# A decoder step on one core: two projections of the first group moved into the step-size chain, history rows written at once, first group written out on TensorE

## The chip, the cores and the metric

The kernel runs on one core of one Trainium2 chip. The metric is the device time of one launch in microseconds (us), the median of several runs; lower is better. Five engines work side by side, each on its own instruction stream and in its own order: TensorE (PE in the profile: matrix products; PEld is its weight load), VectorE (DVE), ScalarE (ACT), GpSimd (POOL) and SyncE (SP, which issues most DMA transfers). They meet at semaphores: an instruction can raise one when it ends, and an engine can wait until one has reached a number.

## The reference, cut to what matters

One layer of a hybrid decoder is computed in float32 for 256 prompt rows and 32 sample rows (8 sequences of 4), together 288 tokens, width 1024. The part that the change touches is the beginning:

```python
h = rmsnorm(x, lw['g_mix'])
proj = h @ lw['w_in']                       # 1024 -> 10272 columns
xbc, dt_raw = proj[..., o3:o4], proj[..., o4:o5]
xbc_c, ssd_buf = causal_dwconv(xbc, ssd_buf0, lw['ssd_conv_w'], lw['ssd_conv_b'])   # 4 taps, history of 3 rows
xbc_c = jax.nn.silu(xbc_c)
dt = jax.nn.softplus(dt_raw + lw['ssd_dt_bias'])
A = -jnp.exp(lw['ssd_A_log'])
a = dt * A;  cum = jnp.cumsum(a, axis=...)   # per chunk, 32 heads
decay_to_end = jnp.exp(cum[:, :, -1:] - cum)
```

An SSD recurrence, an RG-LRU recurrence and gates follow, then the branch and output products, a mixture of 16 experts, and the per-layer embedding gate. All of that is the same before and after.

## The kernel before, in words

The kernel has a prologue, a mixer of eight groups (G = 8), the branch products, the experts and an end. A group needs ten projections of 128 columns each (numbered 0 to 9; 10 and 11 are projections 0 and 1 of the next group). To get float32 accuracy from the faster matrix format, each 128-column weight block is split: ScalarE writes the high part, `whi` (helper `large`, L722), VectorE subtracts it to get the low part, `wlo` (helper `small`, L1007), and TensorE adds three products for each of eight row blocks (helper `proj`, 24 matmuls, L1464 to L1466). There are two `whi`, two `wlo` and two PSUM banks, so a projection waits for its own `wlo` and for the evacuation of the projection two places before it. ScalarE's helper `evac` waits for projection i, splits the weights of projection i+2 (`large`), and copies projection i into a padded buffer `pads[i]` (L752, L753), to which GpSimd adds the three history rows of the samples (L642). VectorE's `conv` then makes four passes over the padded buffer (L1072, L1074 twice, L1077), and ScalarE applies silu.

Every engine's order is fixed in the code. In the prologue, after the normalised input has been transposed and split, a chain makes the step sizes `dt` and what follows from them. It goes to and fro: VectorE adds the bias (L1014) and takes an absolute value (step "ax", L1016); ScalarE an Exp (step "z", L729); VectorE adds 1 (step "u", L1018); ScalarE an Ln (step "ln", L731, with a table load ahead of it); VectorE a correction with a reciprocal, up to `aT` (L1020 to L1028); TensorE transposes it (L1475, L1477); VectorE copies it out, step "atok" (L1030 to L1033); TensorE makes the running sums (L1482); VectorE copies them, `cumT`, and forms `dteT` (L1036 to L1041); ScalarE an Exp (step "dte", L733, again with a table load); TensorE transposes all into token order (L1489, L1490, step "tm"); VectorE copies that into `TM` (L1050, L1051, step "tm" of its own).

TensorE does projections 0 and 1 ahead of that chain and projections 2 to 9 behind it, in the loop over the groups. VectorE does `small` 0 and 1 ahead of the chain, and behind it small 2, conv 0, small 3, conv 1, small 4, conv 2 and so on. GpSimd waits for the end of the chain ("tm"), writes the five sets of history rows, and then computes `Dg`, a product of 64 x 1152 elements (L645), before it copies rows for the state output. ScalarE's and VectorE's programs have group 0 and group 7 written out and a loop over groups 1 to 6; TensorE's has a loop over groups 0 to 6 and group 7 written out.

Of the kernel before, what the change touches and what calls it, by code (L numbers as in the profile page):

```python
# [23 lines left out]
ACT = mybir.ActivationFunctionType  # L24
# [12 lines left out]
G = 8  # L37
# [118 lines left out]
def build(nc, a):  # L156
    with ExitStack() as ctx:
# [38 lines left out]
        u = sb("u", [P, T])  # L196
# [100 lines left out]
        sp = [arena[:, 4608 + 296 * i:4904 + 296 * i] for i in range(5)]  # L297
        aT = arena[0:H, 6249:6537]
        dteT = arena[0:H, 6537:6825]
# [55 lines left out]
        pe_pro = Steps(sem("pe_pro"), [f"x{k}" for k in range(KC)] + ["par", "hist", "rms", "dt", "atok", "cum", "tm"])  # L355
        act_pro = Steps(sem("act_pro"), [f"sq{k}" for k in range(KC)] + ["rs", "A"] + [f"hh{k}" for k in range(KC)] + ["z", "ln", "dte"])
# [272 lines left out]
        def _(pool):  # L629
# [3 lines left out]
            pool.wait_ge(dve_pro.sem, dve_pro.at("tm"))  # L633
            pool.wait_ge(pe_pro.sem, pe_pro.at("tm"))
            with pool.Fori(0, G) as g:
# [7 lines left out]

                pool.wait_ge(CU_ready.sem, CU_ready.at(g, -3))
# [51 lines left out]
        def _(act):  # L696
# [31 lines left out]
            act.wait_ge(dve_pro.sem, dve_pro.at("ax"))  # L728
            ch.step(act_f(sp[2], sp[1], ACT.Exp, scale=-1.0), act_pro, "z")  # L729
            act.wait_ge(dve_pro.sem, dve_pro.at("u"))  # L730
            ch.step(act_f(sp[4], sp[3], ACT.Ln), act_pro, "ln")  # L731
            act.wait_ge(dve_pro.sem, dve_pro.at("dteT"))
            ch.step(act_f(dteT, dteT, ACT.Exp), act_pro, "dte")  # L733

            act.sem_inc(silu_done.sem, 4)
            act.sem_inc(T_free.sem, 1)
            act.sem_inc(CB_free.sem, 1)

# [6 lines left out]
            def evac(g, i):  # L745

                act.wait_ge(projected.sem, projected.at(g, i + 1))
                large(g, i + 2)
                n = i % 10
                act.wait_ge(conv_done.sem, conv_done.at(g, i + 1 - 5 if i < 10 else n + 1))  # L750
                act.wait_ge(stashed.sem, stashed.at(g, i + 1 - 5 if i < 10 else n + 1))
                ch(act_f(pads[n][:, 3:SMP], bP[n % 2][:, 0:NP], ACT.Copy))  # L752
                ch.tell(act_f(new_tokens(pads[n], 3), samples(bP[n % 2][:, NP:T]), ACT.Copy), proj_free, i + 1)  # L753
# [4 lines left out]
            def group(g, first, last):  # L758
# [27 lines left out]
                evac(g, 2)  # L786
# [56 lines left out]

            evac(0, 0)
            evac(0, 1)
            ch.enter(0, 11)
# [124 lines left out]
        def _(dve):  # L971
# [31 lines left out]
            def small(g, b):  # L1003

                s = b % 10 % 5
                dve.wait_ge(w_large.sem, w_large.at(g, b + 1))
                v.tensor_tensor(wlo[b % 2][:], wflat(s), whi[b % 2][:].bitcast(F32), ALU.subtract).then_inc(w_small.sem, 1)  # L1007

            small(0, 0)
            small(0, 1)  # L1010

# [6 lines left out]
            ch.step(v.tensor_scalar(sp[3], sp[2], 1.0, None, ALU.add), dve_pro, "u")  # L1018
            dve.wait_ge(act_pro.sem, act_pro.at("ln"))
# [8 lines left out]
            ch.step(v.tensor_scalar(aT, sp[0][0:H, 0:T], Acol, -1.0, ALU.mult, ALU.mult), dve_pro, "aT")  # L1028
            dve.wait_ge(pe_pro.sem, pe_pro.at("atok"))
# [22 lines left out]
            dve.sem_inc(conv_done.sem, 5)  # L1052
# [33 lines left out]
            small(0, 2)  # L1086
            conv(0, 0, C_SW, 32, C_SB, 0)
            small(0, 3)
# [330 lines left out]
        def _(pe):  # L1419
# [52 lines left out]
            proj(0, 1)  # L1472
            pe.wait_ge(dve_pro.sem, dve_pro.at("aT"))
# [9 lines left out]
            ins.then_inc(pe_pro.sem, 1)  # L1483
            pe.wait_ge(act_pro.sem, act_pro.at("dte"))
# [11 lines left out]
            def group(g, last):  # L1496
# [53 lines left out]
                for i in range(2, 6):  # L1550
                    proj(g, i)
# [62 lines left out]
            with pe.Fori(0, G - 1) as g:  # L1614
                group(g, False)
            group(G - 1, True)
# [246 lines left out]
```

## Time and profile before

| What | Value |
|---|---|
| median of 3 runs | 1013.66 us (1012.64 to 1015.18) |
| the profiled execution: its own time, and its span in the trace | 1013.02 us, 1011.2 us |
| TensorE busy | 899.4 us (89%) |
| VectorE busy | 594.5 us (59%) |
| ScalarE busy | 411.9 us (41%) |
| GpSimd busy | 169.8 us (17%) |
| mean granted clock of TensorE | 0.937 of full speed |
| DMA | 188.54 MB, mean 186 GB/s |

Times in the trace run from the span's start; the 1.8 us between the span and the execution's own time lie outside the traced instructions. "Busy" is an average over stages with different limits, so what a change in one place is worth must be read from that place. The granted clock of TensorE has two levels here, 1.00 (2.4 GHz) and 0.50 (1.2 GHz). The end of a matmul is modelled, and successive matmuls overlap: their starts are the safer numbers.

### The profile page before, as it was taken

The numbers are of one execution on the slowest core, as the hardware profiler recorded it, in microseconds if no ns is written. First come the engines' busy times: TensorE is split into PE (matmuls) and PEld (weight loads), VectorE is DVE, ScalarE is ACT, GpSimd is POOL, SyncE is SP. The second block draws the span as 40 slices with busy tenths as digits, with TensorE's granted clock in tenths as the row PEclk, the third lists the DMA queues.
The fourth block names the chain that finished last, engine by engine and source line by source line (L and its number), as shares of the span: only waits on it lengthen the run. The fifth ranks groups of instructions, "written<-read, shape, count | busy, mean of one in ns | idle before, by whom it ended". The sixth has DMA issues, their size and how long they took to land.

```text
span 1011.2 us, 16515 instructions
## 1 busy us (share of the span) xinstructions
PE 899.4 (89%) x5345; PEld 680.0 (67%) x5345; DVE 594.5 (59%) x1092; ACT 411.9 (41%) x704; POOL 169.8 (17%) x214
## 2 busy tenths in 40 slices
PE   6588997988889897898959999998999999999986
PEld 3488887878788786887839997773444444444464
DVE  2786778788776877878776542345243252333534
ACT  2457564636647464575755331242111111111232
POOL 0045142342513324152310000020000000000000
PEclk9889998989979899997968999998999999999998
DMA  7154552727246172642718522954999999999201
GB/s 200 42 141 124 133 148 62 192 74 204 70 113 186 43 212 67 165 115 77 220 50 227 167 62 64 364 208 148 378 387 387 380 393 385 380 391 374 76 1 47
DMA packets 208603, 188.54 MB, mean 186 GB/s; under 512 B 8000, under 2 KB 166392, under 8 KB 208568
## 3 DMA queue, kind: packets, MB, share of 16 engines
q1 hardware_dynamic: 207352, 187.12, 57.8%
q10 hardware_dynamic: 1216, 0.98, 0.4%
q8 instruction: 18, 0.29, 0.1%
q14 instruction: 17, 0.14, 0.0%
HBM read 176.88 MB, written 11.21 MB: 186 GB/s over the span
## 4 chain that ended last, share of the span: by engine, by line
PE 56%; DVE 16%; ACT 14%; issue 10%; DMA 1%; DVEq 1%; ACTq 0%; SPq 0%
PE bank L1767 12%; PE bank L1795 6%; PE bank L1723 5%; PE bank L1631 5%; PE bank L1730 4%; PE bank L1464 4%; PE bank L1465 3%; PE bank L1466 3%; PE bank L1660 3%; PE bank L1815 3%; DVE yb L1095 3%; PE bank L1635 2%; ACT whi L722 2%; DVE wlo L1007 1%; DVE arena L1092 1%
## 5 line engine op out<-in xcount | busy, mean ns | idle before, releaser
L1464 PE MATMUL bank<-h_hi,whi 128*128 128x288 f32 x640 | 204.1, 319 | 28.8 <-DVE wlo L1007 28.8
L1465 PE MATMUL bank<-h_lo,whi 128*128 128x288 f32 x640 | 196.3, 307 | 0.0
L1466 PE MATMUL bank<-h_hi,wlo 128*128 128x288 f32 x640 | 195.4, 305 | 0.0
L1464 PEld LDWEIGHTS bank<-h_hi,whi 128*128 128x128 f32 x640 | 128.1, 200 | 40.3 <-DVE wlo L1007 35.0
L1361 DVE TENSOR_TENSOR xT<-xT,bank 128x288 f32<-128x288 f32 x128 | 49.5, 449 | 152.3 <-PE bank L1730 152.3
L1465 PEld LDWEIGHTS bank<-h_lo,whi 128*128 128x128 f32 x640 | 127.9, 200 | 1.0
L1007 DVE TENSOR_TENSOR wlo<-wb,whi 128x1024 fp32r<-128x1024 f32 x82 | 119.6, 1459 | 15.1 <-ACT whi L722 7.2
L1466 PEld LDWEIGHTS bank<-h_hi,wlo 128*128 128x128 f32 x640 | 127.6, 199 | 0.0
L722 ACT ACTIVATE whi<-wb 128x1024 fp32r<-128x1024 f32 x82 | 86.8, 1060 | 88.5 <-PE bank L1466 75.5
L935 ACT ACTIVATE Gs<-bank 128x512 f32<-128x512 f32 x16 | 9.6, 597 | 144.9 <-PE bank L1767 144.9
L1631 PE MATMUL bank<-br_hi,whi 128*128 128x288 f32 x192 | 53.3, 303 | 8.9 <-ACT br_hi L862 8.6
L1723 PE MATMUL bank<-pick,htok 96*128 96x256 f32 x240 | 59.0, 386 | 1.1 <-ACT yb L914 1.1
L1795 PE MATMUL bank<-wb,a_T 128*64 128x512 f32 x256 | 58.5, 598 | 0.0
L1723 PEld LDWEIGHTS bank<-pick,htok 96*128 96x128 f32 x240 | 42.9, 190 | 19.0 <-issue 13.0
L1631 PE MATMUL bank<-br_hi,wlo 128*128 128x288 f32 x192 | 52.9, 300 | 0.0
L1074 DVE SCALAR_TENSOR_TENSOR cv<-pad,par,cv 128x312 f32<-128x312 f32 x80 | 43.5, 544 | 9.5 <-DVE cv L1074 0.9
L1767 PE MATMUL bank<-wb,ya 128*64 128x512 f32 x192 | 47.5, 625 | 1.6 <-ACT yb L928 1.6
L1239 DVE TENSOR_TENSOR wlo<-wb,whi 128x1024 fp32r<-128x1024 f32 x22 | 27.0, 1225 | 32.1 <-ACT whi L869 32.1
L1537 PE MATMUL bank<-xbc,arena 128*128 128x4 f32 x256 | 36.5, 275 | 10.2 <-ACT arena L781 10.2
L1767 PE MATMUL bank<-wb,hT 128*64 128x512 f32 x192 | 45.2, 598 | 0.0
L1730 PEld LDWEIGHTS bank<-back,y_sb 64*128 64x128 f32 x272 | 23.5, 186 | 31.6 <-issue 28.2
L1631 PEld LDWEIGHTS bank<-br_hi,whi 128*128 128x128 f32 x192 | 37.4, 195 | 9.9 <-issue 9.4
(366 smaller groups left out, 1550.2 us busy)
## 6 DMA issues: line engine op xcount, KB each, us to landing
wb<-in_w SPq DMA_DIRECT2D x80, 1024.0 KB, 8.4
wb<-in_w_in SPq DMA_DIRECT2D x80, 512.0 KB, 4.1
wb3a<-in_w SPq DMA_DIRECT2D x16, 1024.0 KB, 8.5
arena<-in_state_ssd SPq DMA_DIRECT2D x16, 512.0 KB, 5.8
out_new_ssd_s<-arena SPq DMA_DIRECT2D x16, 512.0 KB, 5.7
wb<-in_w_br_ssd SPq DMA_DIRECT2D x16, 512.0 KB, 3.8
wb<-in_w_br_lru SPq DMA_DIRECT2D x8, 512.0 KB, 4.0
wb<-in_w_out SPq DMA_DIRECT2D x8, 512.0 KB, 3.9
```

The costliest lines, as they stand in the source:

```text
L722: act_f(whi[b % 2][:], wflat(b % 10 % 5), ACT.Copy).then_inc(w_large.sem, 1)
L1007: v.tensor_tensor(wlo[b % 2][:], wflat(s), whi[b % 2][:].bitcast(F32), ALU.subtract).then_inc(w_small.sem, 1)
L1074: ch(v.scalar_tensor_tensor(out=y[:, 0:CVW], in0=x[:, k:k + CVW], scalar=w(k), in1=y[:, 0:CVW], op0=ALU.mult, op1=ALU.add))
L1361: v.tensor_tensor(xT[:, p + 4 * h, :], xT[:, p + 4 * h, :], BACK[2 * (p % 2) + h][:, 0:T], ALU.add).then_inc(cmb_done.sem, 1)
L1464: mm(bP[i % 2][:, 0:T], hi, h_hi[:, k, :], start=(k == 0), stop=False)
L1465: mm(bP[i % 2][:, 0:T], hi, h_lo[:, k, :], start=False, stop=False)
L1466: ins = mm(bP[i % 2][:, 0:T], lo, h_hi[:, k, :], start=False, stop=(k == KC - 1))
L1631: mm(out, w[s % 2][:, k * P:(k + 1) * P], br_hi[:, 8 * t + k, :], start=(k == 0 and w is whi and t < 2), stop=False)
L1723: ins = mm(b[:, SB * (k % 2):SB * (k % 2) + SB], htok[:, c, k * P:(k + 1) * P], pick[:, c, :], start=(c == 0), stop=(c == 2))
L1730: ins = mm(banks[h][:, 0:T], y_sb[r, p * P:(p + 1) * P], back_now[r, :], start=True, stop=True)
L1767: ins = mm(bG[S * h:S * h + S, :], x[:, k, xs_], wpair(m0 + 2 * (k // 4) + h)[:, 512 * (k % 4):512 * (k % 4) + 512], start=(k == 0), stop= ...
L1795: ins = mm(bE[S * h:S * h + S, :], a_T[:, f, :], wpair(m)[:, o:o + 512], start=(f == 0), stop=(f == FC - 1))
```

## The change

Five pieces, shown in the diff. The two projections 2 and 3 of group 0 move into the chain: on TensorE projection 2 stands ahead of the transposes of `aT` and projection 3 between the running sums and the "tm" transposes; on VectorE small 2 stands between "u" and the wait for "ln", and small 3 between `aT` and the wait for "atok"; on ScalarE the evacuations 0, 1 and 2 stand between the three table functions of the chain, and evacuation 2 leaves group 0. GpSimd's history rows wait for "hist" and for a count that VectorE now gives ahead of the chain; the wait for "tm" stands behind them, ahead of `Dg`, inside the loop. TensorE's group 0 is written out, with projections 4 and 5 alone at its head, and the loop runs over groups 1 to 6.

```diff
 # GpSimd
             pool.sem_inc(stashed.sem, 5)
-            pool.wait_ge(dve_pro.sem, dve_pro.at("tm"))
-            pool.wait_ge(pe_pro.sem, pe_pro.at("tm"))
+            pool.wait_ge(dve_pro.sem, dve_pro.at("hist"))
             with pool.Fori(0, G) as g:
...
+                pool.wait_ge(dve_pro.sem, dve_pro.at("tm"))
+                pool.wait_ge(pe_pro.sem, pe_pro.at("tm"))
                 pool.wait_ge(CU_ready.sem, CU_ready.at(g, -3))
                 ch.tell(eng.tensor_tensor(Dg, ...
 # ScalarE
             large(0, 1)
             act.sem_inc(proj_free.sem, 2)
-            act.wait_ge(dve_pro.sem, dve_pro.at("ax"))
-            ch.step(act_f(sp[2], sp[1], ACT.Exp, scale=-1.0), act_pro, "z")
-            act.wait_ge(dve_pro.sem, dve_pro.at("u"))
-            ch.step(act_f(sp[4], sp[3], ACT.Ln), act_pro, "ln")
-            act.wait_ge(dve_pro.sem, dve_pro.at("dteT"))
-            ch.step(act_f(dteT, dteT, ACT.Exp), act_pro, "dte")
-            act.sem_inc(silu_done.sem, 4)
-            act.sem_inc(T_free.sem, 1)
-            act.sem_inc(CB_free.sem, 1)
...
                 silu(0)
-                evac(g, 2)
+                if not first:
+                    evac(g, 2)
                 silu(1)
                 evac(g, 3)
...
+            act.wait_ge(dve_pro.sem, dve_pro.at("ax"))
+            ch.step(act_f(sp[2], sp[1], ACT.Exp, scale=-1.0), act_pro, "z")
             evac(0, 0)
+            act.wait_ge(dve_pro.sem, dve_pro.at("u"))
+            ch.step(act_f(sp[4], sp[3], ACT.Ln), act_pro, "ln")
             evac(0, 1)
+            evac(0, 2)
+            act.wait_ge(dve_pro.sem, dve_pro.at("dteT"))
+            ch.step(act_f(dteT, dteT, ACT.Exp), act_pro, "dte")
+            act.sem_inc(silu_done.sem, 4)
+            act.sem_inc(T_free.sem, 1)
+            act.sem_inc(CB_free.sem, 1)
             ch.enter(0, 11)
             group(0, True, False)
 # VectorE
             small(0, 0)
             small(0, 1)
+            dve.sem_inc(conv_done.sem, 5)
...
             ch.step(v.tensor_scalar(sp[3], sp[2], 1.0, None, ALU.add), dve_pro, "u")
+            small(0, 2)
             dve.wait_ge(act_pro.sem, act_pro.at("ln"))
...
             ch.step(v.tensor_scalar(aT, sp[0][0:H, 0:T], Acol, -1.0, ALU.mult, ALU.mult), dve_pro, "aT")
+            small(0, 3)
             dve.wait_ge(pe_pro.sem, pe_pro.at("atok"))
...
-            dve.sem_inc(conv_done.sem, 5)
             dve.sem_inc(y_done.sem, 1)
...
-            small(0, 2)
             conv(0, 0, C_SW, 32, C_SB, 0)
-            small(0, 3)
 # TensorE
             proj(0, 0)
             proj(0, 1)
+            proj(0, 2)
             pe.wait_ge(dve_pro.sem, dve_pro.at("aT"))
...
             ins.then_inc(pe_pro.sem, 1)
+            proj(0, 3)
             pe.wait_ge(act_pro.sem, act_pro.at("dte"))
...
-            def group(g, last):
+            def group(g, first, last):
...
-                for i in range(2, 6):
+                for i in range(4 if first else 2, 6):
                     proj(g, i)
...
-            with pe.Fori(0, G - 1) as g:
-                group(g, False)
-            group(G - 1, True)
+            group(0, True, False)
+            with pe.Fori(1, G - 1) as g:
+                group(g, False, False)
+            group(G - 1, False, True)
```

The order of the instructions shows three places. The first is VectorE in the middle of the chain. `arena` is the memory of the chain's buffers, `kc` a small table for the other recurrence, `Dt` the first copy of step "atok". Before:

```order
L1018 TENSOR_SCALAR arena<-arena 128x296
L1020 TENSOR_SCALAR arena<-arena 128x296
L1021 RECIPROCAL arena<-arena 128x296
L1022 SCALAR_TENSOR_TENSOR arena<-arena 128x296
L1025 TENSOR_SCALAR kc<-arena 128x8
L1028 TENSOR_SCALAR arena<-arena 32x288
L1030 COPY Dt<-bank 128x16
```

In the changed kernel the same stretch of VectorE reads (line numbers move by one to four):

```order
L1020 TENSOR_SCALAR arena<-arena 128x296
L1008 TENSOR_TENSOR wlo<-wb,whi 128x1024
L1023 TENSOR_SCALAR arena<-arena 128x296
L1024 RECIPROCAL arena<-arena 128x296
L1025 SCALAR_TENSOR_TENSOR arena<-arena 128x296
L1028 TENSOR_SCALAR kc<-arena 128x8
L1031 TENSOR_SCALAR arena<-arena 32x288
L1008 TENSOR_TENSOR wlo<-wb,whi 128x1024
L1034 COPY Dt<-bank 128x16
```

Two splits of weights (`wlo`) have come into the chain: one behind "u", one between `aT` and `Dt`.

The second place is VectorE behind the chain, from the copies into `TM` on; `cv` is the convolution's result. Before:

```order
L1050 COPY TM<-bank 128x3x64
L1051 COPY TM<-bank 96x3x32
L1007 TENSOR_TENSOR wlo<-wb,whi 128x1024
L1072 TENSOR_SCALAR cv<-pad,par 128x312
L1074 SCALAR_TENSOR_TENSOR cv<-pad,par,cv 128x312 x2
L1077 SCALAR_TENSOR_TENSOR cv<-pad,par,cv 128x312
L1007 TENSOR_TENSOR wlo<-wb,whi 128x1024
L1072 TENSOR_SCALAR cv<-pad,par 128x312
L1074 SCALAR_TENSOR_TENSOR cv<-pad,par,cv 128x312 x2
L1077 SCALAR_TENSOR_TENSOR cv<-pad,par,cv 128x312
L1007 TENSOR_TENSOR wlo<-wb,whi 128x1024
```

In the changed kernel VectorE has there:

```order
L1054 COPY TM<-bank 128x3x64
L1055 COPY TM<-bank 96x3x32
L1075 TENSOR_SCALAR cv<-pad,par 128x312
L1077 SCALAR_TENSOR_TENSOR cv<-pad,par,cv 128x312 x2
L1080 SCALAR_TENSOR_TENSOR cv<-pad,par,cv 128x312
L1075 TENSOR_SCALAR cv<-pad,par 128x312
L1077 SCALAR_TENSOR_TENSOR cv<-pad,par,cv 128x312 x2
L1080 SCALAR_TENSOR_TENSOR cv<-pad,par,cv 128x312
L1008 TENSOR_TENSOR wlo<-wb,whi 128x1024
```

The first split behind the chain is now that of projection 4, and it stands behind two whole convolutions.

The third place is ScalarE from the splits of projections 0 and 1 on. L729, L731 and L733 are the chain's Exp, Ln and Exp. Before:

```order
L722 ACTIVATE whi<-wb 128x1024 x2
L729 ACTIVATE arena<-arena 128x296
L731 ACT_TABLE_LOAD
L731 ACTIVATE arena<-arena 128x296
L733 ACT_TABLE_LOAD
L733 ACTIVATE arena<-arena 32x288
L722 ACTIVATE whi<-wb 128x1024
L752 ACTIVATE pad<-bank 128x256
```

In the changed kernel ScalarE's stretch up to the second table load of the chain reads:

```order
L723 ACTIVATE whi<-wb 128x1024 x2
L836 ACTIVATE arena<-arena 128x296
L723 ACTIVATE whi<-wb 128x1024
L742 ACTIVATE pad<-bank 128x256
L743 ACTIVATE pad<-bank 128x8x4
L839 ACT_TABLE_LOAD
L839 ACTIVATE arena<-arena 128x296
L723 ACTIVATE whi<-wb 128x1024
L742 ACTIVATE pad<-bank 128x256
L743 ACTIVATE pad<-bank 128x8x4
```

A whole evacuation (split of projection 2's weights and two copies) now stands between the Exp and the Ln; two more follow the Ln.

## Rows read from the trace of the kernel before

**Rows 1.** page, chain that ended last: share of the span by engine

```profile
PE 56%; DVE 16%; ACT 14%; issue 10%; DMA 1%; DVEq 1%; ACTq 0%; SPq 0%
```

**Rows 2.** TensorE by stretch: from:to us, length, busy (instructions), granted clock, DMA, GB/s

```profile
34.00:40.70 6.70, 6.66 (x48) 1.00 0.60 159
40.70:45.00 4.30, 0.55 (x7) 1.00 0.00 0
45.25:58.50 13.25, 6.95 (x41) 0.50 0.15 40
59.00:86.00 27.00, 26.75 (x193) 1.00 0.68 165
```

**Rows 3.** timeline, TensorE: start us, us, instruction, idle before it and releaser

```profile
34.00 0.40 PE L1464 MATMUL bank<-h_hi,whi 128*128 128x288 f32 x1 [1.40 <-DVE wlo L1007]
...
45.61 1.47 PE L1482 MATMUL bank<-cst,arena 128*64 128x128 f32 x6 [1.30 <-DVE arena L1033]
...
50.34 0.47 PE L1489 MATMUL bank<-cst,arena 32*128 32x32 f32 x3 [3.26 <-ACT arena L733]
...
55.03 0.61 PE L1464 MATMUL bank<-h_hi,whi 128*128 128x288 f32 x1 [2.68 <-DVE wlo L1007]
...
60.18 0.40 PE L1464 MATMUL bank<-h_hi,whi 128*128 128x288 f32 x1
...
63.53 0.40 PE L1464 MATMUL bank<-h_hi,whi 128*128 128x288 f32 x1
...
66.88 0.40 PE L1464 MATMUL bank<-h_hi,whi 128*128 128x288 f32 x1
```

**Rows 4.** timeline, ScalarE

```profile
37.19 1.28 ACT L731 ACT_TABLE_LOAD   x1 [0.50 <-DVE arena L1018]
...
49.84 0.44 ACT L733 ACTIVATE arena<-arena 32x288 f32<-32x288 f32 x1
...
63.72 1.06 ACT L722 ACTIVATE whi<-wb 128x1024 fp32r<-128x1024 f32 x1 [0.67 <-PE bank L1466]
...
65.08 0.20 ACT L753 ACTIVATE pad<-bank 128x32 f32<-128x32 f32 x1
...
76.72 1.28 ACT L800 ACT_TABLE_LOAD   x1
...
78.01 0.50 ACT L800 ACTIVATE rr<-bank,par 128x288 f32<-128x288 f32 x1
```

**Rows 5.** timeline, VectorE

```profile
44.43 0.17 DVE L1030 COPY Dt<-bank 128x16 f32<-128x16 f32 x1 [0.73 <-PE bank L1477]
...
52.86 0.26 DVE L1051 COPY TM<-bank 96x96 f32<-96x96 f32 x1
...
53.75 1.23 DVE L1007 TENSOR_TENSOR wlo<-wb,whi 128x1024 fp32r<-128x1024 f32 x1 [0.64 <-DVE TM L1051]
...
54.89 0.44 DVE L1072 TENSOR_SCALAR cv<-pad,par 128x312 f32<-128x312 f32 x1
...
57.11 3.02 DVE L1007 TENSOR_TENSOR wlo<-wb,whi 128x1024 fp32r<-128x1024 f32 x1
...
150.25 1.47 DVE L1095 SCALAR_TENSOR_TENSOR yb<-yb,par,arena 128x288 f32 x1 [0.62 <-DVE yb L1095]
```

**Rows 6.** timeline, GpSimd

```profile
56.94 2.10 POOL L645 TENSOR_TENSOR arenaR<-hTR,hT 64x1152 fp32r<-64x1152 f32 x1 [0.33 <-POOL pad L642]
...
147.41 4.00 POOL L680 TENSOR_TENSOR arena<-arena,ex 128x1024 f32<-128x1024 f32 x2 [0.34 <-POOL arenaR L672]
```

**Rows 7.** timeline, TensorE, group 0 (first two) and group 7

```profile
71.80 0.40 PE L1464 MATMUL bank<-h_hi,whi 128*128 128x288 f32 x1
...
75.09 0.65 PE L1566 MATMUL bank<-u,wg 128*128 128x288 f32 x2
...
485.75 0.40 PE L1464 MATMUL bank<-h_hi,whi 128*128 128x288 f32 x1
...
489.05 0.65 PE L1566 MATMUL bank<-u,wg 128*128 128x288 f32 x2
```

## The prediction

> **What bounds the kernel now.** I read the chain that ended last first: TensorE holds 56% of it [rows 1], but shares over the whole span say nothing of one stage, so I went to TensorE by stretch, and the reader is to see four pictures there [rows 2]: projections 0 and 1 at the full clock (6.66 us busy of 6.70), a nearly empty stretch, one at half the clock (0.50, which is 1.2 GHz) and half empty, and then 26.75 us of work in 27.00 us at the full clock. The change works in the two poor stretches. The TensorE timeline [rows 3] shows what ends them: the "tm" transposes wait 3.26 us for ScalarE's Exp, and projection 2 starts at 55.03 after 2.68 us of waiting for its `wlo`. Then projections follow one another without idle time: 60.18, 63.53, 66.88. So the end of group 0 is set by the moment at which TensorE starts projection 5 (66.88): from there it is busy until beyond 86. Nothing in the groups behind gives time back, as each hands its work on through the same chain; a shift of projection 5 is, to first order, the shift of the end.
>
> **The chain in the change.** I follow it from "ax", where nothing is different yet.
>
> The Ln moves. Before, its table load starts at 37.19 [rows 4]. Now ScalarE first does evacuation 0. Projection 0 starts at 34.00 and takes 3.35 us at the full clock, as 63.53 to 66.88 shows [rows 3], so it ends at 37.35; in the steady rhythm an evacuation begins 0.2 us after that point (63.72 against 63.53) and ends 1.56 us later (65.08 + 0.20 - 63.72) [rows 4]. The Ln's load starts at 37.35 + 0.2 + 1.56 = 39.1: the chain is 1.9 us later. Small 2 on VectorE (1.23 us [rows 5]) lies in the wait for that Ln and costs nothing; if the Ln came at once it would cost its 1.23.
>
> Small 3 stands between `aT` and the copies of "atok". VectorE waits 0.73 us there before [rows 5], so of its 1.23 us 0.5 remain. The chain is now 2.4 us late: the running sums, which end at 45.61 + 1.47 = 47.08 before [rows 3], end at 49.5, and the Exp "dte", which ends at 49.84 + 0.44 = 50.28 [rows 4], ends at 52.7.
>
> Projection 3 starts on TensorE at 49.5, ahead of "tm", which TensorE can't pass by. At the full clock it takes 3.35 us and ends at 52.85, just behind the Exp. Begun at the low clock, as projection 2 was, it takes 60.18 - 55.03 = 5.15 us and ends at 54.65. Before, the clock was down 4.5 us after projection 1 had ended (between 45.00 and 45.25, after 40.7 [rows 2]). Projection 2 now fills TensorE to 44.05; if the clock goes as late after that as after projection 1, it goes at about 48.5, a little ahead of projection 3, which would start low and end high. I take the middle, 53.75. From the first "tm" transpose to the end of the copies into `TM` it takes 53.12 - 50.34 = 2.78 us at the low clock (52.86 + 0.26 [rows 5]); some 2 us of that are matmuls, which I halve at the full clock, an estimate: 1.75 in all. `TM` then is ready at 53.75 + 1.75 = 55.5 against 53.12. Bounds: 52.85 + 1.75 = 54.6 with the full clock throughout, 54.65 + 2.78 = 57.4 with the low one.
>
> **Behind the chain.** Here time is saved on VectorE: small 2 (1.23) and small 3, which took 3.02 [rows 5], are gone. What follows is conv 0, conv 1 and small 4, for which projection 4 waits. Before `TM` and conv there are 0.63 us of semaphore steps (53.12 to 53.75); one of six is moved away: 0.55. A conv takes 57.11 - 54.89 = 2.2 us, of which its first pass is 0.48 and the other three 1.7.
>
> But `Dg` comes with it. GpSimd, free of the history rows, waits for "tm" alone and starts `Dg` some 0.35 us after it (its wait before is 0.33), for 2.10 us [rows 6]. Before, `Dg` ran from 56.94 to 59.04, and small 3, of two SBUF inputs, started at 57.11 and took 3.02 instead of 1.23: it ended about one small after `Dg`. The conv's last three passes also read two SBUF buffers. That such an instruction is held too shows later: L1095, of nearly the size of one of the conv's passes (about 0.55), takes 1.47 us beside L680 of GpSimd (147.41 to 151.41) and ends at 151.72 [rows 5, 6]. I take the hold: the first pass runs, the others start when `Dg` ends, 2.45 us after `TM`, and conv 0 ends 2.45 + 1.7 = 4.15 after it; without the hold 0.55 + 2.2 = 2.75. The hold costs 1.4 us; its bounds are 0 and 2.1, the length of `Dg`.
>
> The Trainium skill, "SBUF — State Buffer", section "Who interferes with whom", says that a VectorE instruction with two SBUF inputs contends with a GpSimd instruction that reads SBUF, and that whichever starts first keeps the port for the whole instruction. The row of 3.02 us agrees, and by the page the sum is as I make it, while a reading by which only copies are held would give 1.4 us less.
>
> Sum: `TM` 55.5 + 4.15 + 2.2 (conv 1) + 1.23 (small 4) + 0.05 = 63.1 for the start of projection 4, against 63.53: 0.4 us gained. But TensorE has then been idle since its "tm" transposes, some 8 us, and it lost the clock before after idle times with little work between them [rows 2]. Projection 4 goes like projection 2 of before: 5.15 us in place of 3.35, 1.8 lost. Projection 5 starts at 68.3 against 66.88. Its `wlo` (conv 2 and small 5, 3.4 us behind small 4, at 66.5) and its bank (evacuation 3, which follows conv 1's silu, by about 64) are there in time. **The sum is +1.4 us.** Bounds for the last term: 0 if the clock stays up, and 1.8.
>
> **What I cost at nothing.** TensorE's first group written out: group 7 is written out before, and from its projection 6 to the gate products it takes 489.05 - 485.75 = 3.30 us where the looped group 0 takes 75.09 - 71.80 = 3.29 [rows 7]; a gain or loss of 0.3 for the group bounds it from both sides. GpSimd's two waits in the loop come eight times, already satisfied after the first; a wait between its operations shows as 0.3 us, so 5 us in all as the far bound, where TensorE needs `Dg` only after its projection 5. The weights of projections 7 and 8 are asked for earlier by SP, behind small 2 and 3, into slots then free; SP's state loads wait for "tm" as before, 2.4 us later, and are needed behind projection 9.
>
> A rule that speaks against the change: the Trainium skill, "ScalarE: Activation LUTs", section "What ACT_TABLE_LOAD costs", gives about 2.66 us for a switch, a drain of 1.38 included. The Ln's load now stands directly behind an evacuation, so by the page an estimate of 1.4 us more would fall on the chain, +2.8 in all. In the trace the load at 76.72 follows work without idle time, takes 1.28, and the next operation starts at 78.01 [rows 4]: no drain shows, and I go by the row.
>
> **The rivals.** First: it does what it seems meant to do. Full clock throughout, no hold: `TM` at 54.6, projection 4 at 54.6 + 2.75 + 2.2 + 1.23 + 0.05 = 60.85, projection 5 at 64.2: -2.7 us. For it speaks that the work removed from behind the chain is real; against it stand the idle stretch ahead of projection 4, which no part of the change fills, and the row of 3.02.
> Second: no hold, or the clock returns early in projection 4. Without the hold alone the sum is 1.4 - 1.4 = 0. The conv's passes are not small 3, which speaks for it; L1095 against.
> Third, the slower side: projection 3 keeps TensorE at the low clock while "dte" waits. It then ends at 54.65, the transposes stay slow, `TM` is ready at 57.4, projection 4 starts at 65.0 and ends at 70.2: +3.3 us. Each microsecond by which `TM` is late is one of the end, so it passes 3 us, and decides, when `TM` is later than 57.1. For it speaks that the clock was low in all of 45.25 to 58.50 [rows 2]; against, that TensorE is busier now ahead of it.
> Fourth, the change doesn't do what it says: the written-out group meets some cost or gain in fetching its code that group 7 does not show; I give no more than 2 us either way.
>
> **How the numbers follow.** The profiled execution took 1013.02 us, 0.64 under the median 1013.66. The sum gives 1014.4 from the one and 1015.1 from the other; I say 1014.7. About 0.3%, 3 us, is what a measurement of this kernel can tell from no change: faster means below 1010.6, slower above 1016.7. Chances: forecast 0.55; first rival 0.10 (1010.3 to 1011.0, half of it measured as faster); second 0.18 (1012 to 1014); third 0.12 (1016.3 to 1017.0, mostly slower); fourth 0.05, split. Faster 0.08, same 0.79, slower 0.13. The range leaves out the far half of the first and the upper part of the third: 1011.3 to 1017.0.
>
> **What would show it.** In the trace after: the Ln's load at 39.1; `TM` at 55.5; the first conv's middle passes stretched beside `Dg`; TensorE idle from about 55 to 63 and projection 4 at half the clock for most of its length; projection 5 at 68.3. I am wrong if projection 4 starts before 61.5, or runs at the full clock, or if group 0's end moves by more than projection 5's start.

## The result, and the profile after

The changed kernel takes 1016.61 us (median of 15 runs, 1015.27 to 1020.85) against 1014.33 us of the kernel before (15 runs, 1012.52 to 1015.38) on the same chip: a ratio of 1.003, 95% interval 1.0022 to 1.0039. By the medians it is 2.3 us slower; the ratio stands for 3.0 us, its interval for 2.2 to 4.0. Forecast were 1014.7 us, from a sum of +1.4 us, and "no change". The profiled execution of it took 1016.98 us, its span is 1015.1 us. Projection 0 starts 0.23 us earlier in its trace (at 33.77 instead of 34.00); where a time of after is set against one of before, 0.23 us are added, and "from projection 0 on" means the difference to that start.

TensorE's share of the chain that ended last is what it was, VectorE's has grown from 16% to 18% [rows 1]:

```profile
PE 56%; DVE 18%; ACT 12%; issue 10%; DVEq 1%; DMA 1%; ACTq 0%; SPq 0%
```

TensorE by stretch in the changed kernel (from:to, length, busy of each engine with instructions, then granted clock, DMA, GB/s), to be read beside [rows 2]:

```profile
40.50:44.00 3.50, 3.12 (x24) 2.89 (x22) 3.23 (x4) 1.96 (x5) 0.00 (x0) 1.00 0.56 150
44.00:48.00 4.00, 0.88 (x10) 0.73 (x11) 3.31 (x11) 1.24 (x3) 0.00 (x0) 1.00 0.09 8
48.00:51.30 3.30, 3.30 (x16) 2.91 (x14) 2.13 (x7) 0.97 (x1) 0.00 (x0) 0.50 0.54 152
51.50:55.00 3.50, 3.26 (x36) 2.74 (x34) 0.47 (x3) 0.56 (x2) 0.00 (x0) 1.00 0.00 0
58.70:63.00 4.30, 0.00 (x0) 0.00 (x0) 4.05 (x8) 2.41 (x4) 1.60 (x5) 0.50 0.00 0
63.40:68.40 5.00, 4.94 (x20) 4.94 (x21) 4.75 (x10) 2.20 (x5) 1.62 (x2) 0.50 0.76 150
```

The stretch from 40.5 to 55 has filled up, all but the 4 us from 44 on. But there is a new hole behind it, in which TensorE does nothing at all, and behind the hole 5 us of work at half the clock (0.50 in both stretches). The TensorE timeline names the hole (8.70 us of waiting for a `wlo`) and dates the rest, projections 3, "tm", 4, 5 and the product behind them, called CB from here on:

```profile
48.79 0.61 PE L1465 MATMUL bank<-h_hi,whi 128*128 128x288 f32 x1
...
53.35 0.34 PE L1492 MATMUL bank<-cst,arena 32*128 32x32 f32 x3
...
63.46 0.61 PE L1465 MATMUL bank<-h_hi,whi 128*128 128x288 f32 x1 [8.70 <-DVE wlo L1008]
...
69.00 0.29 PE L1465 MATMUL bank<-h_hi,whi 128*128 128x288 f32 x1
...
72.19 0.27 PE L1559 MATMUL bank<-xbc 128*128 128x128 f32 x1
```

ScalarE, with the Ln behind a whole evacuation and no gap ahead of its table load:

```profile
38.67 0.20 ACT L743 ACTIVATE pad<-bank 128x32 f32<-128x32 f32 x1
38.89 1.28 ACT L839 ACT_TABLE_LOAD   x1
40.19 0.45 ACT L839 ACTIVATE arena<-arena 128x296 f32<-128x296 f32 x1
...
51.62 0.45 ACT L843 ACTIVATE arena<-arena 32x288 f32<-32x288 f32 x1
```

VectorE, from small 3 in the chain to small 4 behind conv 1:

```profile
45.36 1.23 DVE L1008 TENSOR_TENSOR wlo<-wb,whi 128x1024 fp32r<-128x1024 f32 x1
46.51 0.17 DVE L1034 COPY Dt<-bank 128x16 f32<-128x16 f32 x1
...
48.96 0.45 DVE L1040 COPY cumT<-bank 32x288 f32<-32x288 f32 x1 [1.34 <-PE bank L1484]
...
55.27 0.25 DVE L1055 COPY TM<-bank 96x96 f32<-96x96 f32 x1
56.16 2.02 DVE L1075 TENSOR_SCALAR cv<-pad,par 128x312 f32<-128x312 f32 x1 [0.64 <-DVE TM L1055]
58.22 1.13 DVE L1077 SCALAR_TENSOR_TENSOR cv<-pad,par,cv 128x312 f32<-128x312 f32 x2
59.38 0.55 DVE L1080 SCALAR_TENSOR_TENSOR cv<-pad,par,cv 128x312 f32<-128x312 f32 x1
59.97 0.44 DVE L1075 TENSOR_SCALAR cv<-pad,par 128x312 f32<-128x312 f32 x1
...
62.18 1.22 DVE L1008 TENSOR_TENSOR wlo<-wb,whi 128x1024 fp32r<-128x1024 f32 x1
```

And GpSimd beside it, which began `Dg` 0.26 us before conv 0:

```profile
55.90 2.10 POOL L646 TENSOR_TENSOR arenaR<-hTR,hT 64x1152 fp32r<-64x1152 f32 x1 [19.29 <-PEq L1497]
```

The first pass of conv 0 takes 2.02 us, that of conv 1, three rows on, 0.44: `Dg` costs VectorE 1.6 us. CB starts at 72.19, which is 38.42 us from projection 0 on, against 70.18 - 34.00 = 36.18 in the kernel before: group 0 is 2.24 us late. That this is so near to the 2.28 us between the medians is partly luck: CB of the groups 1 to 7 stands 1.35 to 2.61 us late in these two traces, and the two traced executions end 3.96 us apart (1016.98 and 1013.02).

### The profile page after: what moved, and what is told of

It reads as the page before. It is cut to its first block, busy times and chain, and to the rows that moved or that the text cites. A ratio compares the mean times of both kernels' runs of the same rounds, so it can differ in the third digit from the quotient of the medians.

```text
span 1015.1 us, 16494 instructions
## 1 busy us (share of the span) xinstructions
PE 900.5 (89%) x5345; PEld 681.9 (67%) x5345; DVE 594.4 (59%) x1092; ACT 411.8 (41%) x704; POOL 168.6 (17%) x214
## 4 chain that ended last, share of the span: by engine, by line
PE 56%; DVE 18%; ACT 12%; issue 10%; DVEq 1%; DMA 1%; ACTq 0%; SPq 0%
PE bank L1771 12%; PE bank L1799 6%; PE bank L1727 5%; PE bank L1635 5%; PE bank L1734 4%; PE bank L1465 4%; PE bank L1466 3%; PE bank L1467 3%; PE bank L1819 3%; PE bank L1664 3%; DVE yb L1096 3%; PE bank L1639 2%; DVE wlo L1008 2%; DVE cv L1077 2%; ACT whi L723 2%
```

## The experiments

The theory (A): the change costs what it delays group 0 by; the delay is made of a late chain, of `Dg`'s hold and of projection 4 at the low clock, and the written-out group costs nothing. The rivals: the written-out group or the early history rows cost something themselves, or something late in the program does. The sixteen kernels are in one table; each was timed side by side with the kernel before on the same chip. "CB" and "p product" are the starts of CB in group 0 and of the first product with the p rows (the per-layer embedding's input; L1717 in before) in the one profiled execution, in us from projection 0 on; such a single execution can stand some two microseconds off its kernel's median (e4: 1019.58 against 1017.40). The times are differences of medians, and can differ from the ratio by most of a microsecond, a small one in its sign.

| Kernel | us, less before beside it | ratio, 95% interval | CB | p product |
|---|---|---|---|---|
| before | - | - | 36.18 | 626.6 |
| changed | +2.3 | 1.003 [1.0022, 1.0039] | 38.42 | 630.5 |
| e1 written out only | -0.1 | 1.0002 [0.9993, 1.001] | 36.19 | 627.6 |
| e2 `Dg` behind conv 1 | +2.0 | 1.0025 [1.0016, 1.0034] | 36.53 | 629.6 |
| e3 kept warm | +2.0 | 1.0019 [1.0009, 1.0029] | 36.35 | 630.1 |
| e4 splits in the chain | +3.0 | 1.0034 [1.0021, 1.0047] | 34.24 | 633.5 |
| e5 written out, delayed | +2.5 | 1.0025 [1.0017, 1.0034] | 37.61 | 630.6 |
| e6 before, p rows early | -0.2 | 0.9998 [0.9989, 1.0006] | 36.07 | 626.2 |
| e7 changed, p rows early | +3.8 | 1.0034 [1.0023, 1.0046] | 38.59 | 628.9 |
| e8 warm, p rows early | -0.4 | 1.0004 [0.9994, 1.0013] | 36.36 | 627.0 |
| e9 projection 3 behind "tm" | +3.5 | 1.0036 [1.0023, 1.0049] | 38.07 | 629.8 |
| e10 `Dg` late, warm, p early | +1.8 | 1.0018 [1.0008, 1.0028] | 39.44 | 629.6 |
| e11 p rows late | +6.2 | 1.0066 [1.0053, 1.008] | 36.17 | 632.2 |
| e12 splits, warm, p early | +0.3 | 0.9999 [0.9984, 1.0014] | 35.64 | 626.3 |
| e13 Ln first | +1.9 | 1.0023 [1.0012, 1.0033] | 37.85 | 628.7 |
| e14 Ln first, warm, `Dg` early | **-3.8** | **0.9972 [0.9958, 0.9985]** | 34.95 | 623.9 |
| e15 warm, p_sample first | +3.1 | 1.0036 [1.0022, 1.0049] | 36.38 | 630.1 |
| e16 helps without the moves | +0.7 | 1.0007 [0.9997, 1.0017] | 36.15 | 627.9 |

**The written-out group alone (e1), and a delay alone (e5).** e1 takes from the change only TensorE's `group(0, True, False)` ahead of the loop. e5 adds to that a bare delay, by matmuls whose result is overwritten; the later "warm" versions have the same line in other places:

```diff
                 for i in range(2, 6):
                     proj(g, i)
+                if first:
+                    for _ in range(3):
+                        mm(bCB[:, 0:T], ident, xT[:, 0, :], start=True, stop=True)
```

> The kernel before, with one edit: TensorE's group 0 written out (all projections where they were). My theory (the loss comes from `Dg` holding the first convolution and from projection 4 at the low clock, and the written-out code costs nothing): the time of before, 1014.3 within 0.7 us. Rival (the code of the written-out group costs time in being fetched): 1015.5 to 1017, most of the 2.3 us by which the change was slower.

> The kernel before with group 0 written out, and three more matmuls of 128 columns (their results are overwritten) on TensorE between projection 5 and CB of group 0: a delay of 2.0 us there (3 x 0.69 us at the most) and nothing else of the change. Theory A (what group 0 loses is carried to the end, and the change costs by its delay alone): 1016.2 to 1016.5, ratio 1.002, about what the changed kernel takes. Theory B (the end does not follow group 0's position; something of the change itself costs later): within 0.5 us of the kernel before, 1013.9 to 1014.9, though the marker CB of group 0 stands 2 us later.

e1 costs nothing, as forecast.

In e5 the delay came out at 37.61 - 36.19 = 1.42 us and not at 2.0, and the kernel lost 2.5 (1016.72 against 1014.21; 1.7 to 3.4 by the interval). So a delay of group 0 is enough to make a loss of this size, with nothing of the change in the kernel; and it costs more than itself. In the traces that shows already at the next CB: that of group 1 stands 2.97 us later than in e1 (93.56 against 90.59 from projection 0 on), and ahead of it TensorE runs at the low clock where it does not in e1 (e1's line stands further down):

```profile
106.00:110.00 4.00, 4.00 (x18) 3.90 (x17) 3.86 (x6) 0.69 (x1) 0.00 (x0) 0.50 0.08 16
```

**The hold (e2) and the low clock (e3).** e2 lets GpSimd wait for conv 1 before `Dg`; e3 gives TensorE ten of those matmuls in its hole:

```diff
 # e2, GpSimd
                 pool.wait_ge(dve_pro.sem, dve_pro.at("tm"))
+                pool.wait_ge(conv_done.sem, conv_done.at(0, 2))
 # e3, TensorE
+            for _ in range(10):
+                mm(bCB[:, 0:T], ident, xT[:, 0, :], start=True, stop=True)
             group(0, True, False)
```

> The changed kernel, with GpSimd's `Dg` waiting until conv 1 has ended, so that it runs beside later passes for which nobody waits yet. My theory: the first pass of conv 0 takes 0.44 us instead of 2.02, projection 4 starts about 1.6 us earlier (61.9 instead of 63.5), and the time falls by 1.6 us, to 1015.0. Rival (the chain's lateness of 2.4 us and the code are the whole loss): no change, 1016.6.

> The changed kernel, with ten matrix products of 128x128 by 128x288 added on TensorE between the end of the chain and projection 4; their results go to a bank that is written over before it is read, and they read data that is there already. They take some 6.9 us and end before projection 4 can start. My theory: the clock stays at its upper level, projection 4 takes 3.3 us instead of 5.4, and the time falls by 2.0 us, to 1014.6. Rival (projection 4's clock doesn't matter, since something behind it is late too): no change, 1016.6.

Both repairs work in group 0: CB comes 1.9 and 2.1 us earlier than in the changed kernel. Neither shows at the end. In e2 the hold has only moved, to the first pass of conv 2, as VectorE and GpSimd show:

```profile
58.32 0.44 DVE L1076 TENSOR_SCALAR cv<-pad,par 128x312 f32<-128x312 f32 x1
...
61.68 2.23 DVE L1076 TENSOR_SCALAR cv<-pad,par 128x312 f32<-128x312 f32 x1
```

```profile
60.98 2.74 POOL L647 TENSOR_TENSOR arenaR<-hTR,hT 64x1152 fp32r<-64x1152 f32 x1 [24.41 <-DVE cv L1081]
```

It costs nothing there (CB and the gate product stand 0.35 us behind e1's alike), but at the end of its group 0 TensorE's clock is low for longer than in e1, and CB of group 1 is nearly as late as in the changed kernel (92.48 against 92.81 from projection 0 on; 90.59 in e1). So the hold's price shows in group 0; no run shows it in the time. The stretches of e2, then of e1:

```profile
102.00:106.00 4.00, 4.00 (x20) 3.71 (x20) 2.54 (x4) 0.69 (x1) 0.44 (x3) 0.59 0.02 4
106.00:110.00 4.00, 4.00 (x20) 4.00 (x20) 3.75 (x9) 0.00 (x0) 0.00 (x0) 0.55 0.48 131
```

```profile
102.00:106.00 4.00, 4.00 (x19) 3.71 (x19) 2.96 (x5) 0.68 (x1) 0.41 (x2) 0.59 0.00 0
106.00:110.00 4.00, 4.00 (x28) 3.79 (x28) 3.75 (x9) 1.52 (x3) 0.00 (x0) 0.99 0.46 131
```

e3 stands within 0.2 us of e1's places up to the output product (613.02 and 613.04) and loses its 2 us behind that. There TensorE waits for the p rows, 0.34 us in e1, 1.33 in e3, and in e3 the clock falls behind the wait (mean 0.72 from 636 to 642; 1.00 in e1).

**The p rows (e6, e7, e8, e11, e15).** Their loads were moved: in e6 to e8 in front of the second half of w_out's loads, in e11 behind two loads of 512 KB (on e1; the expectation speaks of one), in e15 with the last of the three first (on e3).

```diff
 # e6 to e8, SyncE; blk are the three loads of the p rows
+            sp_.wait_ge(br_small.sem, br_small.at(0, 6))
+            blk
             for i in range(4):
                 load(6 + i, wblk(6 + i), w_out[:, :, (4 + i) * P:(5 + i) * P])
             sp_.wait_ge(b_done.sem, b_done.at(3, 6))
-            blk
```

> The kernel before with the loads of the p rows issued in front of the second half of w_out's loads instead of behind it. In the trace of before TensorE waits 0.63 us for them ahead of the transposes of p's rows. Theory A (that wait is where group 0's delay is paid or given back): 0.3 to 0.6 us faster, 1013.8. Rival (the loads move the wait to w_out's own blocks): no change, or 0.5 us slower.

> The changed kernel with the loads of the p rows issued in front of the second half of w_out's loads. In the changed kernel TensorE waits 1.13 us for them, and TensorE's clock falls behind the wait. Theory that 2 us of the loss sit in that stage: 1014.6 to 1015.6, that is 1 to 2 us of the 2.3 back. Rival (the loss is group 0's, and the stage's wait only moves): 1016.4, no change.

> The changed kernel with both: ten matmuls ahead of group 0 that keep TensorE busy, and the loads of the p rows in front of the second half of w_out's loads. With the ten matmuls alone every mark of groups 0 to 7 stood where it stands in the kernel before with group 0 written out, and the 2 us came back at the wait for the p rows. Theory that this wait takes them: 1013.6 to 1014.4. Rival (something else late in the program takes them): 1016.2.

> The kernel before with group 0 written out, and one load of 512 KB put ahead of the p rows' loads on their queue, so that these land later. TensorE's wait for them was 0.34 us in that kernel's trace, 1.33 us in the changed kernel with ten matmuls. If this wait is a place where time is lost beyond the wait itself (TensorE's clock falls behind it): the wait becomes 2 to 3 us and the time 1016.5 to 1018.5. Rival (other work covers it): 1014.3, no change.

> The changed kernel with ten matmuls ahead of group 0, and of the p rows' three loads the one of p_sample issued first and not last; nothing else moves. With the ten matmuls alone every mark up to the output product stood as in the kernel before, TensorE waited 1.33 us for the p rows, and the time was 1016.3. If that wait took the 2 us: the wait falls under 0.5 us and the time is 1014.0 to 1014.8. Rival (the wait is not where they go): 1016.0 to 1016.6.

e7 against e8 is the cleanest pair: measured side by side on one chip, the same kernel but for ten matmuls, 1018.01 against 1013.84. The low clock behind the hole is worth all of the loss once the p rows don't interfere. e7 itself says that the p rows are not what the change costs by: without their wait it is no faster than with it. e6 says that the kernel before loses nothing there: its wait of 0.63 us is gone and its time the same. And since e8 has the early history rows too and is no slower than before, no loss is left for these. e11 and e15 show what that wait does when it grows. In e15 the marks of group 0 and of the output product are those of e8 (613.29 and 613.31), and the wait did not fall under 0.5 us as forecast: it passed to the other rows, 1.53 us; from there on e15 is 3.1 us behind e8 (663.91 against 660.77 at the p product), and 3.4 us at the end (1017.22 against 1013.84). The wait in e1, in e3, in e15 and in e11:

```profile
636.72 1.16 PE L1683 MATMUL bank<-cst,yb 128*128 128x128 f32 x6 [0.34 <-DMA yb<-in_p_sample]
```

```profile
637.68 1.23 PE L1688 MATMUL bank<-cst,yb 128*128 128x128 f32 x6 [1.33 <-DMA yb<-in_p_sample]
```

```profile
638.14 1.36 PE L1688 MATMUL bank<-cst,yb 128*128 128x128 f32 x6 [1.53 <-DMA yb<-in_p_prompt]
```

```profile
639.89 1.79 PE L1683 MATMUL bank<-cst,yb 128*128 128x128 f32 x6 [3.57 <-DMA yb<-in_p_sample]
```

e11 waits 3.2 us longer than e1 and loses 6.3. So this wait is a second place where microseconds go, and with e8 (e3 with its p rows early: -0.4 instead of +2.0) it is what hid the repair in e3. Why the rows land later in e3 (4.6 us after issue, 3.6 in e1, both issued at 633.0) stays open.

**Which step made the chain late (e9, e13).** e9 moves `proj(0, 3)` behind the "tm" transposes. e13 moves the Ln in front of evacuation 0 and the rest after it:

```diff
 # e13: ScalarE
-            evac(0, 0)
             ... Ln ...
+            evac(0, 0)
             evac(0, 1)
-            evac(0, 2)
             ... Exp "dte" ...
+            evac(0, 2)
 # VectorE: small(0, 2) from behind "u" to behind "aT"; small(0, 3) from there to behind "atok"
 # TensorE: proj(0, 2) from behind proj(0, 1) to behind the sums; proj(0, 3) to behind the "tm" transposes
```

> The changed kernel with projection 3 behind the transposes for TM instead of ahead of them. The trace of the changed kernel shows 4.56 us for projection 3 there, and TM at 55.5 instead of 53.1. If that term is real, TM comes at 51 to 53.2, conv 0 starts about 3 us earlier, and CB of group 0 starts by 70.2 (72.2 in the changed kernel). By the theory that group 0's position decides the end: 1014.0 to 1014.9. Rival (as in the run with Dg behind conv 1, what group 0 gains is given back within it or later): 1016.4.

> The changed kernel with the Ln in front of evacuation 0 again, small 2 behind aT, small 3 in the wait for the sums, projection 2 between the sums and the transposes for TM, projection 3 behind these. Moving projection 3 alone behind the transposes brought TM only 0.5 us earlier (55.0 for 55.5), so the Ln's 1.8 us are to be the root of TM's delay. By that theory the sums' copy starts at 47.4 to 47.9 (48.96 in the changed kernel, 47.18 before), TM is there at 53.5 with projection 2 at the full clock and at 55.3 at the low one. CB of group 0: 70.4 to 72.2, and 1014.3 to 1016.3. Rival (small 2 and 3 in VectorE's chain are the root): the sums' copy at 48.5 or later, TM at 55 or later, 1016.5.

e9 fell short: `TM` came 0.3 us earlier from projection 0 on (55.01 - 33.59 against 55.52 - 33.77). The "tm" transposes wait for "dte" anyway, and without projection 3 ahead of them they run slowly again: from the first of them to `TM` it takes 55.01 - 52.24 = 2.77 us, as in the kernel before, where the changed kernel takes 2.17:

```profile
52.24 0.47 PE L1491 MATMUL bank<-cst,arena 32*128 32x32 f32 x3 [3.26 <-ACT arena L843]
```

In e13 the Ln's load starts 3.22 us from projection 0 on, where it was 5.12 in the changed kernel and 3.19 before:

```profile
36.59 1.28 ACT L838 ACT_TABLE_LOAD   x1 [0.50 <-DVE arena L1020]
```

And the copy of the sums starts at 46.95, 13.58 from projection 0 on; it was 15.19 in the changed kernel and 13.18 before:

```profile
46.95 0.45 DVE L1040 COPY cumT<-bank 32x288 f32<-32x288 f32 x1 [0.30 <-PE bank L1483]
...
53.95 0.25 DVE L1055 COPY TM<-bank 96x96 f32<-96x96 f32 x1
54.85 2.02 DVE L1075 TENSOR_SCALAR cv<-pad,par 128x312 f32<-128x312 f32 x1 [0.65 <-DVE TM L1055]
```

So the Ln behind the evacuation makes the chain late: 1.6 of its 2.0 us at the sums come back, with the two splits still in the chain. But only 0.6 us of that stand at CB (37.85 against 38.42), and the time cannot be told from the changed kernel's (1.0023 and 1.003, with intervals that overlap). What is left in its trace is projection 2 at the low clock (0.51 and 0.58 in the stretches from 44 to 51.5), the hold, and projection 4 at the low clock.

**Versions that try for the gain (e4, e10, e12, e14, e16).** e4 puts small 4 into the wait ahead of `TM`, evacuation 3 behind "dte", and lets GpSimd start `Dg` when VectorE has written `eye2` (and TensorE's "tm" is done), ahead of the copies into `TM`. e12 is e4 with seven matmuls ahead of CB and the p rows early. e10 is e2 and e8 together.

> The changed kernel, with small 4 put into VectorE's wait ahead of the "tm" copies, evacuation 3 put behind the Exp "dte" on ScalarE, small 5 put behind conv 0, and `Dg` waiting for the "tm" transposes and its own inputs instead of the copies into `TM`. My theory: TensorE does projection 4 directly behind the chain at about 55.6 and projection 5 at about 60.5; the convolutions run on without splits between them, and projection 6 starts at 69.5 to 71 instead of 73.8. Time 1012.3 to 1014.0, below the kernel before or equal to it. Rival (the written-out code or the late chain costs 2 us wherever the projections stand): not below 1015.

> The changed kernel with Dg behind conv 1, ten matmuls ahead of group 0 and the p rows' loads early. Without the hold (1.6 us) and without the low clock in projections 4 and 5, CB of group 0 starts at 68.4, which is 1.6 earlier than with the matmuls alone. If the end follows: 1012.2 to 1012.6, the change's intended gain at last. Rival (group 0 is then bound elsewhere, by VectorE's passes or the weights' loads): 1013.8, as in the run with matmuls and early p rows.

> The kernel with small 4 in the dt chain's wait, evac 3 behind dte and Dg early, with seven matmuls (3.5 us) between projection 5 and CB of group 0, where TensorE stood idle for 4 us and ran at the low clock afterwards, and with the p rows' loads early. If the low clock was all that ate the gain of 2.6 us at CB (67.57 for 70.18 in before): Yg of group 0 at 72.5 for 75.09, and 1011.3 to 1012.0, below both kernels. Rival (VectorE bounds the rest of group 0): Yg at 74 or later, and 1013.5 to 1015.

e4 brings CB to 34.24, but TensorE stands still for 3.99 us ahead of CB, projection 6 runs for the most part at half the clock behind that (mean 0.60 from 67.5 to 76), and the gate product comes at 75.55 - 33.33 = 42.22 instead of 41.09. e12 repairs that (73.63 - 32.97 = 40.66), but its median is no better than before's, where 1011.3 to 1012.0 were expected; its runs lie from 1008.95 to 1016.78. e10 missed both its theory (1012.2 to 1012.6) and its rival (1013.8): 1015.10. Its profiled execution, one of its slowest, has the low clock already in projections 0 and 1 (0.72 from 34 to 40) and so a late chain (the sums' copy at 51.15), so the trace does not say why; that stays open.

e14 is e13 with three helps: matmuls that fill TensorE's idle time (five behind projection 1, seven ahead of group 0), `Dg` early as in e4, and the p rows early. e16 has such helps and none of the moves (five matmuls behind projection 1, four ahead of group 0, the p rows early).

> As the run with the Ln first, with five matmuls behind projection 1 and seven ahead of group 0 to keep the clock up, Dg's wait moved ahead of the copies into TM, and the p rows' loads early. If delay of the chain, hold and low clock are all that stood against the change: TM at 53.4, conv 0 held for 0.9 us, projection 4 at 60.6, CB of group 0 at 67.4 (70.18 before), and 1010.9 to 1012.0, below both kernels. Rival (later stretches at the low clock or other waits take it back): 1013 to 1015.

> The kernel before with the helps of the last version alone and nothing of the change: five matmuls behind projection 1, four ahead of group 0, the p rows' loads early. If the 3.8 us of the last version (1010.35) came from the clock and the p rows: 1010.5 to 1011.5. If they came from the moved projections and splits, as the chain of waits of before says (projections 3 and 4 there wait for VectorE's splits, at 60.13 and 63.48, whatever the clock): CB of group 0 stays at 70.2, and 1013.7 to 1014.2.

e14 takes 1010.35 us, 3.8 less than the kernel before (1.5 to 4.3 by the interval), and beats both kernels; e16 gains nothing. So the helps alone don't make the gain: it takes the moved projections and splits, where they don't stand in the chain's way and the clock stays up behind them. e14 changes all of this at once, so the share of each is not shown; in its trace 1.2 us of the gain stand at CB (34.95 against 36.18) and 2.8 at the p product. In e14 the hold is 1.30 - 0.44 = 0.9 us, as the first pass of conv 0 meets only the end of `Dg`, and the stretch with projection 4 has the full clock:

```profile
55.47 1.30 DVE L1076 TENSOR_SCALAR cv<-pad,par 128x312 f32<-128x312 f32 x1 [0.65 <-DVE TM L1056]
```

```profile
58.00:62.00 4.00, 2.84 (x12) 1.90 (x10) 3.83 (x7) 2.75 (x6) 1.12 (x3) 1.00 0.01 2
62.00:65.40 3.40, 3.35 (x24) 3.23 (x25) 3.26 (x6) 2.19 (x5) 1.58 (x2) 1.00 0.68 178
```

It did not get there as expected in all: `TM` was there at 54.8, not 53.4 (projection 2 still ran at the low clock, 0.63 and 0.50 from 44 to 51.5), and CB at 68.7, not 67.4.

## Why the prediction was wrong, point by point

The chain of causes held. The step that failed is the sum: from `TM` on its terms were all a little short, 0.9 us together at projection 5, and the largest shortfall is the term "projection 4 goes like projection 2 of before: 5.15 us", which measured 5.54. Two more steps made "no change" of what was left. The forecast of 1014.7 us stood on the three runs and the one profiled execution known then (1013.66 and 1013.02), where fifteen runs of the kernel before have a median of 1014.33; that is another microsecond of the 1.9 between 1014.7 and 1016.61. And 3 us was taken as what a measurement can tell, where the interval came out 0.9 us to either side, so that even +1.4 us would have shown. None of the three signs of being wrong came: projection 4 started at 63.69, for most of its length at the low clock, and group 0's end moved by no more than projection 5 (CB of group 1 by 2.30 us, projection 5 by 2.35).

- The Ln's load at 39.1: it came at 38.89 + 0.23 = 39.12, with no gap ahead of it or behind it (the copy ahead ends at 38.87, the load at 40.17, and the Ln starts at 40.19). Right, and e13 shows that this step carries most of the chain's delay.
- The chain 2.4 us late at the sums: it was 2.0 (48.96 + 0.23 - 47.18). Small 3's half microsecond was there: at `Dt` the chain is 46.51 + 0.23 - 44.43 = 2.3 us late. The sums gave 0.3 back, since they began at the full clock (1.18 us instead of 1.47).
- Projection 3 begins low and ends high: 0.50 up to 51.3, 1.00 from 51.5, 4.56 us. Right, but it cost only 0.3 us (e9): "dte" ends at 52.07 in any case, and projection 3 pays in part for itself with the full clock that the transposes find behind it.
- `TM` at 55.5: 55.75. The estimate of 1.75 us from the first "tm" transpose to `TM` was short by 0.42; it took 55.52 - 53.35 = 2.17 at the full clock. The transposes began 0.17 us earlier than forecast, which leaves +0.25.
- `Dg`'s hold of 1.4 us on conv 0's last three passes: the hold was 1.6 and fell on the first pass, which I had let run since it reads only one SBUF buffer. From `TM` to the end of conv 0 4.41 us instead of 4.15: +0.26. The Trainium skill, "SBUF — State Buffer", section "Who interferes with whom", counts tensor_scalar among the operations that can, where their operands allow it, enter a mode with two ports and then contend with GpSimd. The row of 2.02 us agrees, though no run shows in which mode the pass ran; I had used only that section's sentence on two inputs.
- Conv 1 and small 4: 3.53 us instead of 3.48, +0.05.
- Projection 4 at the low clock 5.15 us: the mechanism was right, the length was not. I took it from projection 2 of before, where the clock rose earlier, after some 15 of the 24 matmuls; here some 21 ran at the low clock, up to 68.60. It took 69.00 - 63.46 = 5.54, +0.39. This is the term that was mis-sized most.
- Projection 5 at 68.3: 69.23, a shift of +2.35 instead of +1.4 (0.25 + 0.26 + 0.05 + 0.39 are the 0.95).
- "A shift of projection 5 is the shift of the end": not shown for the changed kernel, whose 2.24 at CB and 2.28 at the end agree partly by luck, and wrong elsewhere. A delay of 1.42 us cost 2.5 (e5), and 2 us won back in group 0 were lost again behind it (e2, e3).
- The written-out group at nothing: right (e1).

Of the rivals, the first asked for a full clock throughout and no hold; e14 comes closest to that, and its 1010.35 us lie in the rival's 1010.3 to 1011.0. But it wins 1.2 us at CB where the rival had 2.7 at projection 5, and it has the p rows early, so the agreement is partly luck. What it shows is that a gain was there to be had. The second rival had no hold and did not occur. The third had the measured time in its 1016.3 to 1017.0, but not by its cause: it asks for `TM` later than 57.1, and `TM` came at 55.75.

## What to carry to other kernels

Before you fill a waiting engine with work from behind the chain, look on every engine whether that work stands ahead of the chain's own next step: here one evacuation ahead of the Ln on ScalarE made the chain 1.9 us late, while the splits on VectorE and projection 3 on TensorE cost half a microsecond or less each. Work that is moved forward leaves a hole where it was; here TensorE stood idle in it for 8.70 us, projection 4 behind it took 5.54 us instead of 3.35, and that price belongs in the sum at its full length. And when a repair shows in its stage but not at the end, look for the next wait on the same engine, here for the p rows' DMA, before giving the repair up.

## What the runs showed of the hardware that was not expected

- A TENSOR_SCALAR pass with one SBUF input besides its per-partition constants was held for as long as GpSimd's product ran: 2.02 us instead of 0.44 beside a `Dg` of 2.10, 2.23 beside one of 2.74, and 1.30 where `Dg` had begun 0.98 us ahead. In all three the pass ends 0.2 us after `Dg`.
- A delay on TensorE cost more than its length: 1.42 us cost 2.5 (e5; at least 1.7 by the interval), a wait 3.2 us longer cost 6.3 (e11; at least 5.4). In both traces TensorE ran at the low clock where e1 did not: from 106 to 110 the granted clock is 0.50 in e5 and 0.99 in e1, from 642 to 645 it is 0.50 in e11 and 1.00 in e1.
